# VectorE's read of each unit's first product, moved ahead of a stationary tile's low part

## The chip, the cores and the metric

The kernel runs on one core of one Trainium2 chip. The metric is the device time of one launch in microseconds (us), the median of several runs. Five engines work beside each other on the core: TensorE (PE; PEld is its weight load), VectorE (DVE), ScalarE (ACT), GpSimd (POOL) and SyncE (SP, here only a queue of transfers). They meet at semaphores alone.

## The reference

One layer of a decoder trunk on x (256 tokens, 2048 features), all float32:

```python
h = _rmsnorm(x, norm_mix)
b, c, xt, v = split(h @ w_in)                    # 4 x 1024 columns
y_conv = b * causal_depthwise_conv3(c * xt)
y_pool = pool_scale * group_linear(trailing_mean_w(v) - v)
x = x + concat(y_conv, y_pool) @ w_out
h = _rmsnorm(x, norm_mlp)
u = relu(h @ w_up)                               # 2048 -> 8192
x = x + (u * u) @ w_down                         # 8192 -> 2048
return _rmsnorm(x, norm_final)
```

The change lies in the last two products, the MLP.

## The kernel before, in words

**Arithmetic.** Every float32 operand is split in two parts for TensorE: ScalarE copies it to a reduced type (the high part, `w_hi` for a chunk of weights), VectorE subtracts that from the original (the low part, `w_lo`). A product is then high by high, high by low and low by high. A chunk of weights is 128 x 2048 (1 MB). There are four slots for chunks; an item of the stream has slot g % 4. ScalarE's `hi_of` (L793) waits until TensorE has used the item four places earlier (`chunk_used`), VectorE's `lo_of` (L1175) waits for ScalarE's high part, TensorE waits for both.

**The MLP.** The 8192 columns of `w_up` are 16 blocks `t` of 512; each takes 4 chunks, `("up", t, 0)` to `("up", t, 3)` (high parts L397, low parts L400), in banks 0 to 3. From block 2 on, TensorE also works off a unit `d = t - 2` of the down projection, 14 units in all. A unit is Strassen's scheme in Winograd's form: seven products instead of eight, each 128 tokens by 512 columns, on quadrants of `w_down` and on sums of them. They are called `s7_t3`, `a11_b11`, `n6_t2`, `a12_b21`, `s5_t1`, `a22_t4` and `n3_b22`; each is one call of `term` on TensorE, 8 matmuls with the high weights (L579 and L581 in turn) and 4 with the low ones (L585). The weights of such an item are a quadrant, or a sum in `mix_mem` that GpSimd adds up by accumulating transfers (L371) and by one tensor operation (L381). The stationary tiles are in `quads` (`act_b`), eight of them, S7, A11, N6, S5, A12, N3, A22 and A21, each with a high part (ScalarE, `quad_hi`, L818) and a low part (VectorE, `quad_lo`, L1194). Two units share one set: in units with even d ("folding" in the code) VectorE makes most of the set, and in odd ones only what the next set starts with.

**The order on TensorE** in unit d: up chunk 0, a11_b11, up chunk 1, n6_t2, a12_b21, up chunk 2, s7_t3 of unit d+1, s5_t1, up chunk 3, a22_t4, n3_b22. For d = 0 its own s7_t3 stands in front of a11_b11.

**Folding.** a11_b11, n6_t2, s5_t1 and n3_b22 of a unit grow in one PSUM bank (NT, that is bank 4). After each of them VectorE reads the bank and adds it to or subtracts it from the residual `x`: `fold` (L1205). So TensorE may not begin n6_t2 before VectorE has folded a11_b11:

```python
up_chunk(t, 1)
pe.wait_ge(folded, fold_count(d, "a11_b11"))
term("n6_t2", d, N6, NT, False)
```

All folds are counted by one semaphore, in VectorE's order. s7_t3 has a bank of its own (5 or 6), which a22_t4 goes on with.

**Order by hand.** Nothing plans the order: each engine's list is written out, and an engine does its list strictly in turn. SyncE's list is tied to VectorE's: a load into a slot of `w_raw` waits until VectorE has made the low part of what lay there. In unit d these are, in turn, up chunk 0, the quadrant in slot 2, up chunk 1, the base of the next sum, the quadrant for a12_b21 in slot 3, up chunks 2 and 3, and the quadrant for n3_b22 in slot 3, which waits for a12_b21's low part. GpSimd's list waits for the low parts of s7_t3, a11_b11 and n6_t2.

Of the kernel before, what the change touches and what calls it, by code (L numbers as in the profile page):

```python
# [15 lines left out]
NT = 4  # L16
# [63 lines left out]
def build(nc, x_t, x_rows, w_stream, w_quads, pool_w, params, g_final, out):  # L80
    F32, F32R = mybir.dt.float32, mybir.dt.float32r
    ALU, ACT = mybir.AluOpType, mybir.ActivationFunctionType

    ctx = ExitStack()
    with ctx:
# [142 lines left out]
        def fold_count(d, term):  # L228

            if term == "s7_t3":  # L230
                return 1 if d == 0 else fold_count(d - 1, "a12_b21") + 1
            if d + 1 < SEVENS:
                ends = {"s5_t1": 5, "n3_b22": 6, "a22_t4": 7}
            else:
                ends = {"s5_t1": 4, "a22_t4": 5, "n3_b22": 6}
            return 1 + 7 * d + ({"a11_b11": 1, "n6_t2": 2, "a12_b21": 3} | ends)[term]
# [5 lines left out]
        def x_quad(d, t, n):  # L242

            at = BLOCK_COLS * (2 * (d % 2) + n)
            return x[:, t, at:at + BLOCK_COLS]

        def bank_b(d):
            return NT + 1 + d % 2
# [661 lines left out]
        def _(dve):  # L910
# [262 lines left out]
            def lo_of(g, raw):  # L1173
                dve.wait_ge(hi_ready, g + 1)
                dve.tensor_tensor(out=w_lo[:, g % 4, :], in0=raw, in1=w_hi[:, g % 4, :].bitcast(F32),  # L1175
                                  op=ALU.subtract).then_inc(lo_ready, 1)

            def up_lo(t, c):
                lo_of(ITEM["up", t, c], w_raw[:, c % 2, :])

            def add_up(t):

                to = up_values(t)
                dve.wait_ge(cross_ready, IN_CROSSES + t + 1)
                dve.tensor_tensor(out=to[:, :, :], in0=bank_halves(1 if t == 1 else 0, 0),  # L1185
                                  in1=cross[:, :, :], op=ALU.add).then_inc(summed, 1)
                dve.wait_ge(summed, turn(FIRST_UP) + t + 1)
                dve.wait_ge(inv_rms_ready, 2)
                dve.scalar_tensor_tensor(out=to[:, :, :], in0=to[:, :, :], scalar=0.0, in1=by_token(),  # L1189
                                         op0=ALU.max, op1=ALU.mult).then_inc(value_ready, 1)  # L1190

            def quad_lo(s, g, src):
                dve.wait_ge(quad_hi_ready, quad_count(s, g))
                dve.tensor_tensor(out=quad_lo_of(g), in0=src, in1=quad_hi_of(g).bitcast(F32),  # L1194
                                  op=ALU.subtract).then_inc(quad_ready, 1)
                dve.wait_ge(quad_ready, quad_count(s, g))

            def fold(term, d, bank, t, n, op):

                dve.wait_ge(chunk_used, ITEM[term, d] + 1)  # L1200
                count = fold_count(d, term)
                if count > 1:
                    dve.wait_ge(folded, count - 1)
                to = x_quad(d, t, n)
                dve.tensor_tensor(out=to, in0=to, in1=ps[:, bank, :], op=op).then_inc(folded, 1)  # L1205
# [3 lines left out]
            def made(op):  # L1209
                op.then_inc(part_ready, 1)  # L1210
                parts[0] += 1
                dve.wait_ge(part_ready, parts[0])

            def make_s7():
                made(dve.tensor_tensor(out=part_2, in0=held[:, :, 0:P], in1=held[:, :, P:S],
                                       op=ALU.subtract))
# [9 lines left out]
            for t in range(LEAD, UPS):  # L1226
                d, s = t - LEAD, (t - LEAD) // 2
                folding = d % 2 == 0
                if d:
                    fold("s5_t1", d - 1, NT, 1, 1, ALU.subtract)  # L1230
                up_lo(t, 0)
                if d == 0:
                    lo_of(ITEM["s7_t3", 0], sums[0])
                add_up(t - 1)
                lo_of(ITEM["a11_b11", d], w_raw[:, 2, :])
                dve.wait_ge(squared, t)
                if folding:
                    made(dve.tensor_tensor(out=part_0, in0=val[:, :, P:S], in1=held[:, :, P:S],
                                           op=ALU.subtract))
                    made(dve.scalar_tensor_tensor(out=part_1, in0=held[:, :, 0:P], scalar=-1.0,  # L1240
                                                  in1=part_0, op0=ALU.mult, op1=ALU.subtract))
                elif s + 1 < SLICES - 1:
                    make_s7()
                if d:
                    fold("n3_b22", d - 1, NT, 0, 1, ALU.subtract)
                up_lo(t, 1)
                if d:
                    fold("a22_t4", d - 1, bank_b(d - 1), 1, 0, ALU.add)
                if folding:
                    quad_lo(s, N6, part_1)  # L1250
                    quad_lo(s, S5, part_0)
                    made(dve.scalar_tensor_tensor(out=part_1, in0=part_1, scalar=-1.0,
                                                  in1=val[:, :, 0:P], op0=ALU.mult, op1=ALU.subtract))
                elif s + 1 < SLICES - 1:
                    quad_lo(s + 1, S7, part_2)
                else:
                    quad_lo(s + 1, A21, held[:, :, P:S])
                dve.wait_ge(t2_added, d + 1)
                lo_of(ITEM["n6_t2", d], sums[d % 2])
                if folding:  # L1260
                    quad_lo(s, A12, val[:, :, 0:P])
                lo_of(ITEM["a12_b21", d], w_raw[:, 3, :])
                if d == 0:
                    fold("s7_t3", 0, bank_b(0), 1, 1, ALU.subtract)
                fold("a11_b11", d, NT, 0, 0, ALU.add)
                if folding:
                    quad_lo(s, N3, part_1)
                    quad_lo(s, A22, val[:, :, P:S])
                else:
                    quad_lo(s + 1, A11, held[:, :, 0:P])  # L1270
                up_lo(t, 2)
                if d + 1 < SEVENS:
                    lo_of(ITEM["s7_t3", d + 1], sums[(d + 1) % 2])
                fold("n6_t2", d, NT, 1, 0, ALU.add)
                lo_of(ITEM["s5_t1", d], w_raw[:, 2, :])
                fold("a12_b21", d, NT + 3, 0, 0, ALU.add)
                up_lo(t, 3)
                lo_of(ITEM["a22_t4", d], sums[d % 2])
                if d + 1 < SEVENS:
                    fold("s7_t3", d + 1, bank_b(d + 1), 1, 1, ALU.subtract)  # L1280
                lo_of(ITEM["n3_b22", d], w_raw[:, 3, :])
# [105 lines left out]
```

## Time and profile before

| | |
|---|---|
| median of 3 runs | 973.25 us (970.35, 973.25, 974.61) |
| profiled execution, its own time | 970.65 us |
| its span, first to last instruction | 968.9 us |
| PE busy | 950.2 us (98%) |
| DVE busy | 782.1 us (81%) |
| ACT busy | 526.8 us (54%) |
| POOL busy | 116.3 us (12%) |
| share of the DMA engines in the stretch of the units | 0.89 to 0.91 |
| granted TensorE clock | 0.998 of full speed |

1.75 us of the profiled execution lie outside its span. TensorE's row is almost full, but its matmuls overlap in the records, so busy time alone does not say how dense the stream is; the spacing of starts does. The units take the time from about 335 us to 917 us.

### The profile page before, as it was taken

How to read it: one execution, taken by the hardware profiler on the slowest of the kernel's cores; microseconds unless marked ns; L12 is line 12 of the kernel's file. 1: busy time of each engine (PE TensorE's matmuls, PEld its weight loads, DVE VectorE, ACT ScalarE, POOL GpSimd, SP SyncE). 2: the span in 40 equal slices, each digit the busy share in tenths (PEclk: the TensorE clock that was granted, in tenths of full speed). 3: DMA queues.
4: the chain of work that ended last, by engine and by line, in shares of the span. 5: the costliest groups of instructions: out<-in, count | busy, mean ns of one | idle time of the engine just before them, and what ended most of it. 6: DMA issues, size and time to landing. Idle time of an engine off the chain costs nothing.

```text
span 968.9 us, 12019 instructions
## 1 busy us (share of the span) xinstructions
PE 950.2 (98%) x4920; PEld 815.6 (84%) x4920; DVE 782.1 (81%) x605; ACT 526.8 (54%) x420; POOL 116.3 (12%) x65
## 2 busy tenths in 40 slices
PE   8999999999999999999999999999999999999996
PEld 7888888888888878888888888888888888888885
DVE  6597768664555699899999989989998998998864
ACT  6754335344444566465665556556555655646642
POOL 0000000000000203203020220203212030230000
PEclk9999999999999999999999999999999999999999
DMA  9956452655547598898979889898998989878832
GB/s 341 401 186 249 159 203 93 239 202 189 175 174 247 184 295 245 288 263 265 317 253 293 238 290 278 274 322 238 301 246 274 296 268 315 239 240 225 307 119 88
DMA packets 35763, 237.85 MB, mean 245 GB/s; under 512 B 3968, under 2 KB 4224, under 8 KB 7808
## 3 DMA queue, kind: packets, MB, share of 16 engines
q1 hardware_dynamic: 29232, 190.85, 51.0%
q0 software_dynamic: 6192, 45.09, 23.9%
q10 hardware_dynamic: 288, 1.18, 0.3%
q8 instruction: 37, 0.61, 0.2%
q14 instruction: 14, 0.11, 0.0%
HBM read 235.01 MB, written 2.10 MB: 245 GB/s over the span
## 4 chain that ended last, share of the span: by engine, by line
PE 73%; DVE 11%; issue 11%; DMA 2%; ACT 2%; SPq 0%; ACTq 0%; DVEq 0%
PE ps L397 26%; PE ps L400 14%; PE ps L488 9%; PE ps L579 6%; PE ps L581 6%; PE ps L585 6%; PE ps L623 4%; DVE w_lo L1175 3%; DMA w_raw<-w_stream 2%; DVE x L1205 2%; DVE act_b L1194 1%; ACT w_hi L793 1%; DVE val L1189 1%; DVE val L1185 1%; DVE w_lo L1009 1%
## 5 line engine op out<-in xcount | busy, mean ns | idle before, releaser
L397 PE MATMUL ps<-act_a,w_hi 128*128 128x512 f32 x1472 | 349.7, 390 | 0.0
L1175 DVE TENSOR_TENSOR w_lo<-w_raw,w_hi 128x2048 fp32r<-128x2048 f32 x120 | 324.3, 2702 | 8.3 <-ACT w_hi L793 7.2
L397 PEld LDWEIGHTS ps<-act_a,w_hi 128*128 128x128 f32 x1472 | 274.1, 188 | 55.5
L793 ACT ACTIVATE w_hi<-w_raw 128x2048 fp32r<-128x2048 f32 x120 | 229.4, 1913 | 76.5 <-PE ps L585 53.3
L400 PEld LDWEIGHTS ps<-act_a,w_lo 128*128 128x128 f32 x1472 | 188.6, 191 | 7.0
L400 PE MATMUL ps<-act_a,w_lo 128*128 128x256 f32 x1472 | 191.1, 283 | 0.0
L914 DVE TENSOR_TENSOR w_lo<-w_raw,w_hi 128x2048 fp32r<-128x2048 f32 x52 | 118.5, 2290 | 67.1 <-ACT w_hi L656 66.4
L579 PE MATMUL ps<-w_hi,act_b 128*128 128x512 f32 x392 | 153.9, 393 | 7.3 <-DVE x L1205 7.3
L581 PE MATMUL ps<-w_hi,act_b 128*128 128x512 f32 x392 | 153.3, 391 | 0.0
L656 ACT ACTIVATE w_hi<-w_raw 128x2048 fp32r<-128x2048 f32 x52 | 99.0, 1912 | 63.8 <-PE ps L400 39.0
L1175 DVE TENSOR_TENSOR w_lo<-mix_mem,w_hi 128x2048 fp32r<-128x2048 f32 x42 | 96.2, 2291 | 40.3 <-ACT w_hi L793 39.8
L793 ACT ACTIVATE w_hi<-mix_mem 128x2048 fp32r<-128x2048 f32 x42 | 80.2, 1910 | 80.1 <-PE ps L400 77.4
L381 POOL TENSOR_TENSOR mix_mem<-mix_mem,w_raw 128x2048 f32<-128x2048 f32 x14 | 78.4, 5598 | 249.7 <-DMA w_raw<-w_quads 226.1
L585 PE MATMUL ps<-w_lo,act_b 128*128 128x512 f32 x392 | 104.8, 389 | 0.0
L579 PEld LDWEIGHTS ps<-w_hi,act_b 128*128 128x128 f32 x392 | 73.8, 188 | 22.4 <-DVE x L1205 8.7
L585 PEld LDWEIGHTS ps<-w_lo,act_b 128*128 128x128 f32 x392 | 73.6, 188 | 15.3
L581 PEld LDWEIGHTS ps<-w_hi,act_b 128*128 128x128 f32 x392 | 73.8, 188 | 13.9
L1205 DVE TENSOR_TENSOR x<-x,ps 128x512 f32<-128x512 f32 x98 | 66.7, 680 | 3.0 <-PE ps L585 2.4
L488 PE MATMUL ps<-w_hi,act_b 128*128 128x512 f32 x256 | 68.8, 390 | 0.0
L371 POOL DMA_DIRECT2D mix_mem<-w_quads x28 | 24.5, 876 | 359.1 <-DMA mix_mem<-w_quads 262.5
L488 PEld LDWEIGHTS ps<-w_hi,act_b 128*128 128x128 f32 x256 | 47.8, 188 | 9.7
L807 ACT ACTIVATE cross<-ps 128x1024 f32<-128x1024 f32 x16 | 16.4, 1026 | 54.6 <-PE ps L400 54.6
(103 smaller groups left out, 589.0 us busy)
## 6 DMA issues: line engine op xcount, KB each, us to landing
w_raw<-w_stream SPq DMA_DIRECT2D x108, 1024.0 KB, 6.5
w_raw<-w_quads SPq DMA_DIRECT2D x50, 1024.0 KB, 8.8
mix_mem<-w_quads POOLq DMA_DIRECT2D x28, 1024.0 KB, 10.2
mix_mem<-w_quads SPq DMA_DIRECT2D x14, 1024.0 KB, 4.7
w_raw<-w_quads POOLq DMA_DIRECT2D x14, 1024.0 KB, 10.5
w_raw<-w_stream SPq DMA_DIRECT2D x16, 256.0 KB, 8.2
x<-x_rows SPq DMA_DIRECT2D x2, 1024.0 KB, 15.8
mix_mem<-x_t SPq DMA_DIRECT2D x3, 512.0 KB, 8.5
```

Of the source, the lines that this page charges most:

```text
L381: pool.tensor_tensor(out=sums[d % 2], in0=sums[d % 2], in1=w_raw[:, 2, :], op=ALU.add)\
L397: return pe.matmul(ps[:, bank, :], weights_hi, act, start=first, stop=False)
L400: return pe.matmul(ps[:, bank, 0:S], weights_lo, act[:, 0:S], start=False, stop=last)
L488: mm = pe.matmul(ps[:, NT * parity + t, :], a[:, at:at + P], cols, start=first and i == 0, stop=last and i == 2)
L579: pe.matmul(to, quads[:, quad, k, 0:P], weights_of(w_hi, g, k), start=first and k == 0, stop=False, skip_group_check=not first)
L581: pe.matmul(to, quads[:, quad, k, P:2 * P], weights_of(w_hi, g, k), start=False, stop=False, skip_group_check=not first)
L585: mm = pe.matmul(to, quads[:, quad, k, 0:P], weights_of(w_lo, g, k), start=False, stop=k == CK - 1, skip_group_check=not first)
L656: act.activation(w_hi[:, c, :], w_raw[:, c, :], ACT.Copy).then_inc(hi_ready, 1)
L793: act.activation(w_hi[:, g % 4, :], raw, ACT.Copy).then_inc(hi_ready, 1)
L914: dve.tensor_tensor(out=w_lo[:, c, :], in0=w_raw[:, c, :], in1=w_hi[:, c, :].bitcast(F32), op=ALU.subtract)\
L1175: dve.tensor_tensor(out=w_lo[:, g % 4, :], in0=raw, in1=w_hi[:, g % 4, :].bitcast(F32), op=ALU.subtract).then_inc(lo_ready, 1)
L1205: dve.tensor_tensor(out=to, in0=to, in1=ps[:, bank, :], op=op).then_inc(folded, 1)
```

## The change

In VectorE's list of a unit, the fold of a11_b11 moves up. Before, it stood behind the low part of tile A12 (in even units) and behind the low part of a12_b21's weights; now it stands directly behind the low part of n6_t2's weights. In unit 0 alone the fold of s7_t3, which has to stay ahead of it because of the common count, moves further, to behind the low part of up chunk 1. No instruction is added or removed, and the lists of the other engines stay as they are.

```diff
                 up_lo(t, 1)
                 if d:
                     fold("a22_t4", d - 1, bank_b(d - 1), 1, 0, ALU.add)
+                else:
+                    fold("s7_t3", 0, bank_b(0), 1, 1, ALU.subtract)
                 if folding:
                     quad_lo(s, N6, part_1)
                     quad_lo(s, S5, part_0)
...
                 dve.wait_ge(t2_added, d + 1)
                 lo_of(ITEM["n6_t2", d], sums[d % 2])
+                fold("a11_b11", d, NT, 0, 0, ALU.add)
                 if folding:
                     quad_lo(s, A12, val[:, :, 0:P])
                 lo_of(ITEM["a12_b21", d], w_raw[:, 3, :])
-                if d == 0:
-                    fold("s7_t3", 0, bank_b(0), 1, 1, ALU.subtract)
-                fold("a11_b11", d, NT, 0, 0, ALU.add)
                 if folding:
                     quad_lo(s, N3, part_1)
                     quad_lo(s, A22, val[:, :, P:S])
```

## Rows read from the trace of the kernel before

**Rows 1.** Waits of TensorE, whole span: total us, times, longest us.
```profile
PE ps L579 <- DVE x L1205: 7.3, 7, 2.0
```

**Rows 2.** Windows from stall to stall, first and last of six: length, busy us by engine.
```profile
348.26:432.01 83.75, 82.88 (x424) 70.94 (x424) 77.05 (x52) 48.31 (x34) 15.73 (x8) 1.00 0.91 279
...
767.11:850.92 83.81, 82.92 (x424) 70.94 (x424) 77.10 (x52) 49.42 (x34) 17.33 (x8) 1.00 0.89 276
```

**Rows 3.** Timeline of TensorE in unit 2: start us, us of the merged row.
```profile
420.78 2.08 PE L400 MATMUL ps<-act_a,w_lo 128*128 128x256 f32 x16
422.69 0.40 PE L579 MATMUL ps<-w_hi,act_b 128*128 128x512 f32 x1
...
424.54 1.07 PE L585 MATMUL ps<-w_lo,act_b 128*128 128x512 f32 x4
...
429.07 2.07 PE L400 MATMUL ps<-act_a,w_lo 128*128 128x256 f32 x16
432.01 0.50 PE L579 MATMUL ps<-w_hi,act_b 128*128 128x512 f32 x1 [0.88 <-DVE x L1205]
...
433.99 1.08 PE L585 MATMUL ps<-w_lo,act_b 128*128 128x512 f32 x4
```

**Rows 4.** Timeline of VectorE in unit 2.
```profile
420.56 0.69 DVE L1205 TENSOR_TENSOR x<-x,ps 128x512 f32<-128x512 f32 x1
...
426.14 2.29 DVE L1175 TENSOR_TENSOR w_lo<-mix_mem,w_hi 128x2048 fp32r<-128x2048 f32 x1
428.35 0.69 DVE L1194 TENSOR_TENSOR act_b<-val,act_b 128x512 fp32r<-128x512 f32 x1
...
431.28 0.68 DVE L1205 TENSOR_TENSOR x<-x,ps 128x512 f32<-128x512 f32 x1
431.88 0.69 DVE L1194 TENSOR_TENSOR act_b<-cross,act_b 128x512 fp32r<-128x512 f32 x1
```

**Rows 5.** Timelines of TensorE and of VectorE in unit 0.
```profile
337.88 0.39 PE L579 MATMUL ps<-w_hi,act_b 128*128 128x512 f32 x1
...
344.23 2.07 PE L400 MATMUL ps<-act_a,w_lo 128*128 128x256 f32 x16
348.26 0.50 PE L579 MATMUL ps<-w_hi,act_b 128*128 128x512 f32 x1 [1.96 <-DVE x L1205]
339.42 1.41 DVE L1194 TENSOR_TENSOR act_b<-cross,act_b 128x512 fp32r<-128x512 f32 x2
343.80 0.69 DVE L1194 TENSOR_TENSOR act_b<-val,act_b 128x512 fp32r<-128x512 f32 x1
```

**Rows 6.** Unit 3: VectorE's low part, ScalarE released by a11_b11, TensorE's n6_t2.
```profile
468.67 2.29 DVE L1175 TENSOR_TENSOR w_lo<-w_raw,w_hi 128x2048 fp32r<-128x2048 f32 x1
468.19 0.63 ACT L818 ACTIVATE act_b<-win 128x512 fp32r<-128x512 f32 x1 [0.83 <-PE ps L585]
473.47 0.40 PE L579 MATMUL ps<-w_hi,act_b 128*128 128x512 f32 x1
```

**Rows 7.** Idle times of VectorE later on, from its timeline.
```profile
361.58 2.29 DVE L1175 TENSOR_TENSOR w_lo<-mix_mem,w_hi 128x2048 fp32r<-128x2048 f32 x1 [1.93 <-ACT w_hi L793]
445.38 2.29 DVE L1175 TENSOR_TENSOR w_lo<-mix_mem,w_hi 128x2048 fp32r<-128x2048 f32 x1 [1.96 <-ACT w_hi L793]
```

**Rows 8.** A low part while GpSimd adds; GpSimd's addition, min/median/max ns.
```profile
405.70 6.11 DVE L1175 TENSOR_TENSOR w_lo<-w_raw,w_hi 128x2048 fp32r<-128x2048 f32 x1
L381 POOL TENSOR_TENSOR mix_mem<-mix_mem,w_raw x14: 4617/5526/6595, 327.9 to 864.4; 128x2048 f32<-128x2048 f32 x14
```

**Rows 9.** SyncE's load for n3_b22 in unit 2; SyncE's quadrant loads to landing; TensorE's n3_b22.
```profile
431.39 0.33 SPq L315 DMA_DIRECT2D w_raw<-w_quads  x1
DMA to landing us min/median/max: 4.6/7.3/12.6
456.92 0.39 PE L579 MATMUL ps<-w_hi,act_b 128*128 128x512 f32 x1
```

**Rows 10.** ScalarE's longest wait for a transfer, 400 to 920 us.
```profile
ACT w_hi L793 <- DMA mix_mem<-w_quads: 2.7, 1, 2.7
```

## The prediction

> **What bounds the kernel now.** I read the page's first two parts, then the waits by engine, the windows, and last the timelines of TensorE and VectorE around one place. TensorE's row is full nearly everywhere, so the first question is where it stands still. The view of TensorE's waits has one entry of size: 7.3 us in 7 pieces, all ahead of a term's first matmul (L579) and all ended by a fold (L1205) [rows 1]. The longest, 2.0 us, lies in unit 0; the other six lie at about 0.9 us in units 2, 4, ..., 12. Odd units have none. From one of them to the next the windows are 83.75 to 83.81 us long, all six alike [rows 2]: a period of two units that TensorE's work sets, plus one stall.
>
> The timeline says which fold it is. In unit 2 the low half of up chunk 1 starts at 429.07, and the next matmul, the first of n6_t2, at 432.01 [rows 3]. VectorE's fold there runs from 431.28 to 431.96 [rows 4]; by the order of its list it is that of a11_b11. TensorE goes on 0.05 us after its end. VectorE is not waiting at that point: from the low part of n6_t2's weights at 426.14 on it works without a break. The fold is late only because two other instructions stand ahead of it, A12's low part at 428.35 and that of a12_b21's weights right behind.
>
> **What a stall costs.** A chunk's 16 low matmuls take 1.91 us from their first start to the next instruction's (420.78 to 422.69), so without the wait n6_t2 would begin at 429.07 + 1.91 = 430.98. It begins at 432.01: 1.03 us late. Its first eight matmuls then need 433.99 - 432.01 = 1.98 us where an undisturbed term needs 424.54 - 422.69 = 1.85; the pipeline fills anew, 0.13 us [rows 3]. Together 1.16 us. In unit 0, 344.23 + 1.91 = 346.14 against 348.26 is 2.12 us [rows 5], with the same 0.13 us 2.25 us. Sum: 6 x 1.16 + 2.25 = 9.2 us, if every stall goes fully.
>
> **Does the fold come early enough, in even units?** It now takes the place of A12's low part: start 428.35 [rows 4]. It may start, since a11_b11 was through before up chunk 1 began. Duration 0.68 us, end 429.03, and 0.05 us later TensorE knows. TensorE arrives at 430.98, so 1.90 us are to spare. The stall does not shrink, it goes, and VectorE could be that much later before it came back.
>
> **Unit 0.** Here the fold of s7_t3 goes ahead too. It starts at 339.42, where the low part of N6 started; s7_t3 was through when TensorE began a11_b11 at 337.88, so it does not wait. A fold moves what follows by 0.60 us (431.28 to 431.88 [rows 4]). The low part of n6_t2's weights, followed before by A12's at 343.80, is then done at 344.40, and the fold of a11_b11 runs from 344.40 to 345.08. TensorE arrives at 346.14 [rows 5]: 1.0 us to spare. I count the whole 2.25 us.
>
> **Odd units.** The fold moves ahead of a12_b21's low part, to 468.67. a11_b11 ended just before: ScalarE was released by it at 468.19 [rows 6]. So VectorE passes the wait with 0.48 us in hand. Were it earlier by more than that, it would wait for TensorE, but TensorE needs the fold only at 473.47, more than 4 us after it. Nothing gained, nothing lost.
>
> **What is late next.** What the fold overtakes comes 0.60 us later, and TensorE 1.03 to 1.16 us earlier than before. (1) A12's low part starts at 428.95 and is done at 429.64; a12_b21 begins behind all of n6_t2, whose first eight matmuls alone take 1.85 us, so not before 430.98 + 1.85 = 432.83. (2) The low part of a12_b21's weights runs from 429.67 to 431.96 at 2.29 us; its first use is 1.85 us into the term, not before 434.68: at least 2.7 us to spare. (3) Behind both, VectorE's list is at the same time as before, 431.88, for the sum of durations is unchanged; against TensorE it is 1.16 us later. That lag does not pile up: at 445.38, in the same unit, VectorE has been idle for 1.96 us, ended by ScalarE, which follows TensorE's use of the slots [rows 7]. The idle time becomes 0.8 us and the two stand to each other as before. In unit 0 the idle time is 1.93 us at 361.58 against 2.25 us of gain; 0.3 us of lag go into unit 1. (4) The nearest other fold, that of n3_b22, ends at 421.25 [rows 4] for a term that begins at 422.69 [rows 3], 1.4 us; it hangs on the standing at the last common point and does not move. So nothing in the even unit takes the stall's place, and in unit 1 the 0.3 us fit in 1.4.
>
> **Transfers.** One of them hangs on a moved instruction: SyncE loads n3_b22's quadrant when a12_b21's low part is done, at 431.39 in unit 2 [rows 9], so at 432.0 now. SyncE's entries behind it wait for later low parts that don't move. TensorE begins n3_b22 at 456.92 before, 455.8 now, and needs its low part 1.85 us in, at 457.6. Going back over 6.11 us for a disturbed low part [rows 8] and, generously, as much again for ScalarE's copy ahead of it, the load must land by 445.4, 13.4 us from its issue; the slowest of SyncE's quadrant loads took 12.6 us [rows 9]. GpSimd's orders wait for the low parts of s7_t3, a11_b11 and n6_t2; only in unit 0 is one (n6_t2's) later, by 0.60 us.
>
> **GpSimd beside VectorE.** In each unit one low part takes some 6.1 us where others take 2.29; it lies beside GpSimd's addition, which takes 4.62 us undisturbed [rows 8]. The transfers that start the addition follow VectorE, and the waits that VectorE is held by follow TensorE, so the addition moves by up to 1.16 us against VectorE's list and may fall on the next item. The price by rows: VectorE is held for 3.83 us now and can be held for at most one whole addition, 4.62 us, so 0.8 us more, within the 1.4 us of (4). I take nothing, and keep 0.8 - 0.8 = 0 as the lower and, for six pairs where the margin has gone, 6 x 0.8 = 4.8 us as the upper bound.
>
> The Trainium skill ("Trainium Architecture — The Big Picture", What this means for kernel authors) calls the SBUF port pair of VectorE and GpSimd an exclusive lock and not a split of bandwidth. The trace agrees (6.11 us in place of 2.29 us); by that rule the later of the two waits for the other, and the sum stays at 9.2 us as long as one addition meets one low part per unit. The rule speaks against the change only if the addition got in ahead of n6_t2's low part, and its time is elsewhere in the unit.
>
> **Sum.** 970.65 - 9.2 = 961.4 us for the profiled execution. It is at the low end of the runs shown; from their median, 973.25, it is 964.0. The four executions' middle is 972.0, which gives 962.8. I take 963.5.
>
> **Rivals.**
> (A) All stalls go, as above: 963.5 us, 961 to 966 with the scatter of the runs. Chance 0.76.
> (B) The lag shows elsewhere. VectorE loses 1.16 us per pair against TensorE and has 1.96 us of idle time to absorb it; if the addition above takes its 0.8 us more, nothing is left, and TensorE stands at the following fold or sum. Then some 0.8 us of 1.16 come back in each pair, 4.8 us in all: 968.3 us. For it: the 0.3 us of unit 1. Against: the 1.4 us that must go first. Chance 0.12.
> (C) The transfers pace the units, with the DMA engines 0.89 to 0.91 busy [rows 2]. Then the six stalls are time that would be waited for anyway, and only unit 0's 2.25 us is won: 971.0 us. Against it: the longest wait of ScalarE for a transfer in over 500 us is 2.7 us, once [rows 10]. A fold that is not the last release, so that TensorE stays where it is, would look the same. Chance 0.08.
> (D) Slower: the later load of n3_b22. If that load, not TensorE, set the pace, each of 14 units would get 0.60 us longer and the stalls' end would win nothing: 973.25 + 8.4 = 981.7 us. It decides once the load takes over 13.4 us, against 12.6 at most. Chance 0.04.
>
> **Range and chances.** 0.5% is 4.9 us, about what a measurement of this kernel tells from no change. The range reaches from 960.0 (A from the lowest run, 970.35 - 9.2 = 961.2, and a little scatter) to 968.5, which takes in B; C and D and the ends of A's scatter are left out. Faster by over 0.5%: A, and half of B, whose 4.9 us lie on the line: 0.82. Within 0.5%: the other half, C: 0.14. Slower: D, 0.04.
>
> **What the profile after would show.** Right: no entry of L1205 in TensorE's waits; six windows of 82.6 us between the starts of n6_t2 in even units; the fold of a11_b11 at 0.68 us directly behind n6_t2's low part; VectorE's idle time in even units 0.8 us in place of 1.96; its busy time the same. B would show new waits of TensorE for VectorE and a low part beside the addition over 6.5 us; C, waits of ScalarE for transfers, and windows still near 83.8; D, ScalarE's wait ahead of n3_b22. The prediction is wrong if another semaphore was the late one in the stall, or if VectorE's idle time is not there when the stall is gone.

## The result and the profile after

The changed kernel takes 961.78 us (median of 6 runs: 961.26, 961.37, 961.63, 961.93, 964.38, 964.45), the kernel before beside it 972.83 us (6 runs, 970.35 to 974.87). The ratio is 0.9896, 95% interval 0.9875 to 0.9916, so the change is worth 8.2 to 12.2 us. Forecast were 963.5 us, in a range from 960.0 to 968.5, and a sum of 9.2 us.

TensorE's waits after, whole span (line and releaser, total us, times, longest us), beside the one entry of [rows 1]:

```profile
PE ps L462 <- DVE val L921: 2.9, 1, 2.9
PE ps L422 <- DVE w_lo L1009: 1.2, 2, 0.8
PE ps L521 <- POOL win L364: 1.0, 1, 1.0
```

The entry of the folds is gone; what is left lies ahead of the MLP, before 50 us. The kernel before waits at the same three lines, for 2.0 us at L422, 1.0 us at L521 and, at L462:

```profile
PE ps L462 <- DVE val L921: 0.3, 1, 0.3
```

The windows from one even unit to the next, first and last of six, show what that gives (bounds, length, busy us of PE, PEld, DVE, ACT, POOL, clock, DMA share, GB/s):

```profile
347.16:429.77 82.61, 82.61 (x425) 70.89 (x424) 77.86 (x54) 50.49 (x34) 15.24 (x9) 1.00 0.92 285
...
760.23:842.84 82.61, 82.61 (x426) 70.89 (x424) 77.08 (x52) 49.42 (x34) 15.99 (x9) 1.00 0.92 279
```

Length and TensorE's busy time are now the same number, 82.61; before, 0.9 us were missing in each [rows 2], and they were 83.75 to 83.81 us long. The same place of unit 2 on TensorE:

```profile
429.77 2.08 PE L400 MATMUL ps<-act_a,w_lo 128*128 128x256 f32 x16
431.69 0.40 PE L579 MATMUL ps<-w_hi,act_b 128*128 128x512 f32 x1
...
433.53 1.07 PE L585 MATMUL ps<-w_lo,act_b 128*128 128x512 f32 x4
```

From the low half to n6_t2 it is 1.92 us, where it was 2.94 us [rows 3], and n6_t2's first eight matmuls take 1.84 us, not 1.98. VectorE there, and its idle time later in the unit:

```profile
426.86 2.29 DVE L1175 TENSOR_TENSOR w_lo<-mix_mem,w_hi 128x2048 fp32r<-128x2048 f32 x1
429.07 0.68 DVE L1205 TENSOR_TENSOR x<-x,ps 128x512 f32<-128x512 f32 x1
429.67 0.69 DVE L1194 TENSOR_TENSOR act_b<-val,act_b 128x512 fp32r<-128x512 f32 x1
...
444.91 2.29 DVE L1175 TENSOR_TENSOR w_lo<-mix_mem,w_hi 128x2048 fp32r<-128x2048 f32 x1 [0.77 <-ACT w_hi L793]
```

The fold ends at 429.75, 1.94 us ahead of the matmul that needs it. The idle time is 0.77 us where it was 1.96 us [rows 7]. From the low half of up chunk 1 in unit 0 (347.16 after, 344.23 before) to that of the last up chunk (903.44 after, 909.72 before) the units take 556.28 us instead of 565.49 us: 9.21 us less.

The profiled execution as a whole, 964.38 us against 970.65 us, shows only 6.3 us less, because it reached the units 2.9 us later. That comes from the wait at L462, which is not where the change was made. The wait ends 1.5 us later than in the kernel before's trace (48.15 us against 46.63), and the lower clock behind it costs the rest: the next high half starts at 52.07 us against 49.09, 3.0 us later. Runs 10 to 12 below are about it.

### The profile page after: what moved, and what is told of

It is laid out like the page before. It is cut to its first block, busy times and chain, and to the rows that moved or that the text cites. A ratio compares the mean times of both kernels' runs of the same rounds, so it can differ in the third digit from the quotient of the medians.

```text
span 962.6 us, 12019 instructions
## 1 busy us (share of the span) xinstructions
PE 949.4 (99%) x4920; PEld 816.6 (85%) x4920; DVE 782.5 (81%) x605; ACT 526.9 (55%) x420; POOL 113.0 (12%) x65
## 4 chain that ended last, share of the span: by engine, by line
PE 94%; DMA 3%; DVE 2%; SPq 1%; ACT 0%; issue 0%; ACTq 0%
PE ps L397 34%; PE ps L400 18%; PE ps L581 9%; PE ps L579 9%; PE ps L585 9%; PE ps L488 9%; PE ps L623 5%; DMA w_raw<-w_stream 3%; DVE w_lo L1009 1%; SPq L295 0%; PE ps L422 0%; PE ps L474 0%; DVE act_a L964 0%; DVE w_lo L914 0%; ACT w_hi L656 0%; SPq L280 0%
## 5 line engine op out<-in xcount | busy, mean ns | idle before, releaser
L397 PE MATMUL ps<-act_a,w_hi 128*128 128x512 f32 x1472 | 349.7, 390 | 0.0
L397 PEld LDWEIGHTS ps<-act_a,w_hi 128*128 128x128 f32 x1472 | 274.1, 188 | 55.5
L381 POOL TENSOR_TENSOR mix_mem<-mix_mem,w_raw 128x2048 f32<-128x2048 f32 x14 | 75.1, 5367 | 248.7 <-DMA w_raw<-w_quads 225.2
```

What stands on the lines that cost most here:

```text
L381: pool.tensor_tensor(out=sums[d % 2], in0=sums[d % 2], in1=w_raw[:, 2, :], op=ALU.add)\
L397: return pe.matmul(ps[:, bank, :], weights_hi, act, start=first, stop=False)
```

## The experiments

### Which units pay: runs 1 to 3

Run 1 moves the fold in even units alone, run 2 in unit 0 alone, run 3 in odd units alone. In all three the code behind n6_t2's low part is

```diff
-                fold("a11_b11", d, NT, 0, 0, ALU.add)
+                moved = folding                    # run 2: d == 0; run 3: not folding
+                if moved:
+                    fold("a11_b11", d, NT, 0, 0, ALU.add)
                 if folding:
                     quad_lo(s, A12, val[:, :, 0:P])
                 lo_of(ITEM["a12_b21", d], w_raw[:, 3, :])
+                if not moved:
+                    if d == 0:
+                        fold("s7_t3", 0, bank_b(0), 1, 1, ALU.subtract)
+                    fold("a11_b11", d, NT, 0, 0, ALU.add)
```

and in run 3 the early fold of s7_t3 is taken out too.

> The fold of a11_b11 is moved in even units alone (unit 0 with its s7_t3 fold); in odd units it stays behind the low part of a12_b21's weights. My theory (only even units had a stall, so only they gain): the same as the changed kernel, 9 to 10 us below the kernel before, no wait of TensorE for a fold, windows of 82.6 us from n6_t2 to n6_t2 of the next even unit. Rival (VectorE's order in odd units shares in the gain, or costs): more than 1 us off the changed kernel, seen as windows other than 82.6 us.

961.67 us, ratio to the kernel before 0.9903 (0.9881 to 0.9925), 10.5 us less by the medians, a little over the 9 to 10 expected. No wait for a fold; windows of 82.61 us, and 556.28 us from unit 0 to the last up chunk, as in the changed kernel. The even units are the whole of it.

> Both folds are moved in unit 0 alone. Theory: of the seven stalls one goes, the one of 2.25 us; six waits of TensorE of 0.9 us each stay in units 2, 4, ..., 12 and the windows stay at 83.75 to 83.8 us; time 2 to 2.5 us below the kernel before (about 970.5). Rival C (transfers pace the even units, and only unit 0's share is real): this kernel is as fast as the changed one, 962.

968.62 us, ratio 0.9966 (0.9953 to 0.9978), so 3.6 us less by the medians and not the 2 to 2.5 us expected. In the trace, though, all is as expected: the first window, unit 0 to unit 2, is 82.62 us, the others stay at 83.77, and the way from unit 0 to the last up chunk is 563.21 us, 2.28 us less than before. Rival C, that transfers pace the even units, falls: with their stalls left in, the kernel is 6.8 us slower than the changed one. What did not fit was the median. It came with another thing: these six executions lay between 968.35 and 968.80 us, while those of the kernel before, measured beside them, were spread over 3.9 us (970.55 to 974.47). The fastest of each are 2.2 us apart, as expected; the surplus lies in the slower executions of the kernel before.

> The fold is moved in odd units alone; in even units all stands as in the kernel before. Theory: no gain and no loss, all seven waits stay (7.3 us), time as before within 0.2%. Rival (VectorE, held up for TensorE's a11_b11 by the moved fold, gets later): VectorE idle before L1205 in odd units, and longer stalls in the even units behind them.

972.18 us, ratio 1.000 (0.9988 to 1.0011), all seven waits at 7.3 us. But its trace takes 567.01 us from unit 0 to the last up chunk, with the same waits as the kernel before with 565.49 us. The 1.5 us lie directly behind unit 0's stall. TensorE's timeline there:

```profile
348.17 0.66 PE L579 MATMUL ps<-w_hi,act_b 128*128 128x512 f32 x1 [1.96 <-DVE x L1205]
348.62 0.63 PE L581 MATMUL ps<-w_hi,act_b 128*128 128x512 f32 x1
349.04 0.63 PE L579 MATMUL ps<-w_hi,act_b 128*128 128x512 f32 x1
349.47 0.63 PE L581 MATMUL ps<-w_hi,act_b 128*128 128x512 f32 x1
```

and the windows around it, where the third number from the right is the granted clock:

```profile
347.00:348.00 1.00, 0.00 (x0) 0.00 (x0) 0.90 (x2) 1.00 (x1) 0.00 (x0) 1.00 1.05 188
348.00:349.00 1.00, 0.83 (x2) 0.69 (x3) 0.96 (x3) 0.22 (x1) 0.00 (x0) 0.68 0.90 156
349.00:350.00 1.00, 1.00 (x4) 0.77 (x3) 0.97 (x2) 0.00 (x0) 0.00 (x0) 0.50 0.90 180
350.00:351.00 1.00, 1.00 (x4) 0.81 (x3) 1.00 (x1) 0.00 (x0) 0.00 (x0) 0.50 1.05 246
351.00:352.00 1.00, 1.00 (x4) 0.77 (x4) 1.00 (x2) 0.00 (x0) 0.00 (x0) 0.62 0.91 238
352.00:353.00 1.00, 1.00 (x6) 0.83 (x5) 1.00 (x1) 0.14 (x1) 0.00 (x0) 1.00 1.01 279
```

TensorE has stood for 1.96 us; some 0.2 us after it goes on, the clock is at 0.50, the lower of its two levels (1.2 GHz), and the matmuls start 0.43 us apart instead of 0.23 us, eight times over, 1.6 us in sum. From this stretch's low half to that of unit 2 it is 86.43 us (344.14 to 430.57), in the kernel before's trace, with the same stall at full clock, 84.84 us (344.23 to 429.07): 1.59 us.

### Unit 0's stall alone: run 4

The changed kernel, with `moved = d > 0` in the code of run 1 and s7_t3's fold back in its old place.

> The changed kernel with unit 0 alone put back: there both folds stand where the kernel before had them, so its stall of 2.0 us is back and no other. In the run with the fold moved only in odd units, TensorE's granted clock stood at 0.50 for some 3 us right behind that stall, and the matmuls there started 0.43 us apart in place of 0.23 us; the kernel before's own trace has the same stall at full clock. Theory (the stall in unit 0 costs 2.25 us always, and 1.6 us more in the executions in which the clock drops to the lower level behind it): runs between 963.5 and 965.5, median 964 to 965.5, more scattered than the changed kernel; 6 to 8 us below the kernel before. Rival (the stall costs its 2.25 us and the scatter has its place elsewhere): median 963.7, scatter as in the changed kernel.

965.51 us (963.56, 963.87, 965.31, 965.71, 965.75, 966.48), ratio 0.9924 (0.9907 to 0.9941). The profiled execution is the fastest, 963.56 us, with the stall of 2.0 us and the clock at 1.00 behind it; it is 2.3 us above the fastest of the changed kernel (961.26). The median is 3.7 us above the changed kernel's, between the 2.25 us of the stall alone and the 3.85 us with the lower clock behind it; the scatter ahead of the units (runs 10 to 12 below) is in it too. The rival's 963.7 us is missed by the median, not by the fastest executions. Three executions lie above the 965.5 us expected as the upper end. In the trace the way from unit 0 to the last up chunk is 558.54 us (344.08 to 902.62), 2.26 us more than in the changed kernel: that is the price of this stall at full clock, 2.25 us forecast.

So the stall costs its length always, and more in most executions. That the clock is what the slower four lost is likely and not shown: the run's one trace is of the fastest. The mean granted clock on record for each execution points that way, 0.998 in the two fastest and 0.994 to 0.997 in the other four. But it is a mean over the whole execution, and it can't tell where the clock was low: run 1's fastest execution has 0.995, and its trace shows the lower clock between 8 and 12 us and again behind 945 us, with no loss in the units.

### How much room there is: runs 5 to 8

Run 5 puts the fold behind A12's low part, still ahead of the weights' low part:

```diff
                 lo_of(ITEM["n6_t2", d], sums[d % 2])
-                fold("a11_b11", d, NT, 0, 0, ALU.add)
                 if folding:
                     quad_lo(s, A12, val[:, :, 0:P])
+                fold("a11_b11", d, NT, 0, 0, ALU.add)
                 lo_of(ITEM["a12_b21", d], w_raw[:, 3, :])
```

> In all units the fold stands behind A12's low part but still ahead of the low part of a12_b21's weights: 0.72 us later in even units than in the changed kernel. Theory (1.90 us to spare in even units, 1.0 us in unit 0): the same time as the changed kernel, no wait of TensorE for a fold. Rival (the margin is smaller than worked out from starts and ends): waits of TensorE for L1205 come back, in unit 0 first.

961.45 us, ratio 0.9891 (0.9875 to 0.9908), no wait for a fold, windows of 82.61 us. It is the overtaking of the weights' low part that counts; A12's is not in the way.

Runs 6 to 8 add work to VectorE that nothing uses, a sum over 128x1024 elements (1.22 us by the traces; two of them, with the gap behind, 2.50 us), to an otherwise unchanged kernel:

```diff
+            def extra(n):
+                for _ in range(n):
+                    dve.tensor_reduce(out=ballast[:, :], in_=by_token(), axis=mybir.AxisListType.X,
+                                      op=ALU.add).then_inc(extra_done, 1)
...
+                if folding:
+                    extra(1)          # run 7: extra(2); run 8: extra(2), behind the fold
                 fold("a11_b11", d, NT, 0, 0, ALU.add)
```

> The changed kernel with one more VectorE instruction, a sum of 128x1024 elements that nothing uses, some 1.1 to 1.3 us, ahead of the moved fold in each even unit. Theory (1.90 us to spare in even units, 1.0 us in unit 0): no wait in units 2 to 12, one of 0.1 to 0.3 us in unit 0; time within 0.5 us of the changed kernel. Rival (the margin worked out from the rows is too large): waits of TensorE for L1205 in every even unit.

962.49 us, ratio 0.9895 (0.9874 to 0.9916); no recorded wait for a fold, the windows from unit 2 on 82.62 us. The median is 0.7 us above the changed kernel's, where 0.5 was expected. From unit 0 to unit 2 it is 83.20 us, 0.59 us more than in the changed kernel. Some 0.35 us of it are at the fold: n6_t2 begins at 346.68, 0.25 us after the 344.52 + 1.91 at which it could, and refills for 0.10 us. The other 0.24 us lie ahead of unit 1's first up chunk, which waits for VectorE's sum: the sum ends at 374.31 and TensorE begins at 374.37 instead of 374.27, and refills. It is the place at which run 8 loses its time.

> Two such instructions ahead of the moved fold in each even unit, some 2.4 us, more than the 1.90 us to spare. Theory: the stalls come back at 0.4 to 0.6 us each in six units and 1.4 us in unit 0, each with 0.13 us of refill: 4 to 6 us above the changed kernel. Rival (VectorE has room and TensorE would wait elsewhere): the same time as the changed kernel, or waits in odd units too and more than 8 us.

968.34 us, ratio 0.9957 (0.9945 to 0.9969): 6.6 us above the changed kernel, 4 to 6 expected. TensorE's waits (TensorE's lines are two higher in this kernel, the fold's is L1216):

```profile
PE ps L581 <- DVE x L1216: 4.8, 7, 1.3
```

The timelines of VectorE and of TensorE in its unit 2, the added work first:

```profile
428.67 2.47 DVE L1204 TENSOR_REDUCE ballast<-inv_rms 128x4 f32<-128x1024 f32 x2
431.17 0.69 DVE L1216 TENSOR_TENSOR x<-x,ps 128x512 f32<-128x512 f32 x1
429.09 2.07 PE L402 MATMUL ps<-act_a,w_lo 128*128 128x256 f32 x16
431.91 0.50 PE L581 MATMUL ps<-w_hi,act_b 128*128 128x512 f32 x1 [0.75 <-DVE x L1216]
```

All seven stalls are back. In units 6 to 12 they are 0.47 us by the record and 0.6 us by the starts, as 2.50 - 1.90 gives, and the windows there are 83.37 us, 0.75 us up (0.6, and 0.13 of refill). In units 2 and 4 they are 0.3 us longer than forecast: there VectorE also comes later into the unit.

> The same two instructions directly behind the moved fold in even units, so that the fold is on time and everything after it in VectorE's list is some 2.4 us later. Rival B of the prediction at work: VectorE's idle time of 0.8 us later in the unit is used up and some 1.6 us of lag go into the odd unit, where 1.4 us are to spare ahead of the up chunk that waits for VectorE's sum. Theory: no wait of TensorE in even units, waits of 0.2 to 0.4 us in the six or seven odd ones; 1 to 3 us above the changed kernel. Rival (the lag is absorbed in full): the same time as the changed kernel.

966.97 us, ratio 0.9939 (0.9918 to 0.9960): 5.2 us above the changed kernel, against 1 to 3 expected. The fold is on time and TensorE stands instead in the odd units, ahead of the up chunk that waits for VectorE's sum (the chunk's line, L399 here, is L397 in the changed kernel). The view of the waits holds four of the stalls; by the starts there is one in each of the seven odd units:

```profile
PE ps L399 <- DVE win L1187: 1.9, 4, 1.0
```

In the steady pairs the price is as worked out: windows of 83.03 to 83.15 us, 0.4 to 0.5 us up. Taking 0.13 us of refill off 0.42 leaves 0.29; so of 2.50 us, 0.77 went into idle time and 2.50 - 0.77 - 0.29 = 1.44 us into the room ahead of the sum, 1.4 us forecast. The theory missed the ends: 1.3 us are lost behind unit 0, which has no idle time left, 1.0 us at the end of unit 2, where a low part beside GpSimd's addition takes 6.67 us, and 0.9 us behind unit 12. This is the mechanism of rival B, which needed 2.5 us of added work to show at all.

### The load of n3_b22: run 9

```diff
-                load_quad(w_raw[:, 3, :], d, 3, ITEM["a12_b21", d], raw_loaded[3])
+                load_quad(w_raw[:, 3, :], d, 3, ITEM["up", t, 2], raw_loaded[3])
```

> The changed kernel, but SyncE's load for n3_b22 waits for the low part of up chunk 2 instead of a12_b21's, so it is issued 3 to 4.5 us later in every unit. Rival D of the prediction (a later load of n3_b22 sets the pace) would make every one of 14 units longer: over 40 us in all. Theory (the load has at least 13.4 us, and needs 12.6 at most): time within 0.3% of the changed kernel, windows of 82.6 us, perhaps a longer wait of ScalarE for the transfer.

962.09 us, ratio 0.990 (0.9873 to 0.9927). In unit 2 the load is issued 6.6 us behind the start of up chunk 1's low half (433.39 against 426.80) where the changed kernel issues it 2.9 us behind (432.71 against 429.77), 3.7 us later; the windows stay at 82.61 us. Rival D falls.

### The wait ahead of the units: runs 10 to 12

In run 10 TensorE spreads the first norm (L462) behind the high half of chunk 3 of its block instead of chunk 2; run 12 is the same kernel again, beside run 11, which is the changed kernel again.

```diff
-            gemm_block(1, act_a, 1, norm=0, norm_after=11)
+            gemm_block(1, act_a, 1, norm=0, norm_after=15)
```

> The changed kernel, but the spreading of the first norm by TensorE (L462), where TensorE stood for 2.9 us in the changed kernel's profiled execution with the clock at 0.50 behind it, stands behind the high half of chunk 3 of block 1 instead of chunk 2. Theory: this wait is what separates the executions near 964.4 us from those near 961.5 us; without it all runs lie within 1 us, at 960.5 to 961.8. Rival (VectorE and ScalarE now wait for the norm some 5 us longer, and their later work on the pool branch holds TensorE up): 1 to 5 us slower than the changed kernel, with waits of TensorE in the blocks behind.

960.50 us (959.96, 960.36, 960.63, 960.87), ratio 0.9875 (0.9851 to 0.9899). TensorE has no wait at L462 and none that is new; VectorE stands 4.8 us for what follows the norm, and TensorE does not wait for that.

> The changed kernel once more, beside the next run on the same chip. So far one execution in four of it and of its near copies lay near 964 us and the others at 961 to 962. Theory (the wait at the first norm, and the lower clock behind it, come in some executions): the same picture, median 961.5 to 962, one or two executions at 963.5 or more.

962.58 us (961.20, 962.57, 962.58, 964.04), ratio 0.9905 (0.9888 to 0.9922), 0.6 us above the upper end of what was expected for the median. The profiled execution, 962.57 us, waited 1.4 us at L462.

> The changed kernel with the first norm's spreading behind chunk 3's high half, once more. Theory: no execution over 961.5 us, median 960.3 to 960.8, 1.0 to 1.5 us below the changed kernel in the same call, and TensorE's row without a wait at L462. Rival (the four executions so far were lucky): the same scatter as the changed kernel, executions near 963 to 964 among them.

960.63 us (960.13, 960.30, 960.97, 961.28), ratio 0.9886 (0.9870 to 0.9903), 1.95 us below run 11, measured beside it, where 1.0 to 1.5 were expected; no wait at L462. No execution of the eight went over 961.28 us, while 8 of the 22 of the changed kernel and of the copies with the same units (runs 1, 5, 9, 11) were at 962.5 us or more.

What a long wait there does is in the changed kernel's own trace, first in TensorE's timeline:

```profile
48.15 1.22 PE L462 MATMUL ps<-inv_rms,ones 128*128 128x128 f32 x4 [2.87 <-DVE val L921]
49.03 3.21 PE L400 MATMUL ps<-act_a,w_lo 128*128 128x256 f32 x16
```

and then in the windows of the same stretch:

```profile
46.00:48.00 2.00, 0.00 (x0) 0.00 (x0) 1.90 (x6) 2.00 (x2) 0.00 (x0) 1.00 1.01 422
48.00:50.00 2.00, 1.85 (x8) 1.85 (x9) 1.82 (x2) 0.76 (x3) 0.00 (x0) 0.50 0.77 320
```

2.87 us of waiting, then the clock at 0.50 and a low half of 3.21 us that takes 2.08 us elsewhere. What makes VectorE late there in some executions was not followed further; in this trace the two low parts ahead of the norm start 1.5 us later than in the kernel before's (40.37 against 38.84). The profiled executions line up with it: a wait of 0.7 us or less in three at 961.17 to 961.40 us (runs 1, 5 and 9), 1.4 us in run 11 at 962.57, 2.9 us with the lower clock at 964.38. The start of up chunk 1's low half in unit 0 makes it exact: an execution's time less that start is 617.21 or 617.22 us in all seven traces of these units (the changed kernel, runs 1, 5, 9, 10, 11 and 12) and 626.42 us in the kernel before's. So what these seven differ by, 960.30 to 964.38 us, lies wholly ahead of the units, and the change itself is 9.2 us in each.

## Why the prediction was right

**Which fold, and what a stall costs.** Right. With the fold moved no such wait is left, and the sum of 6 x 1.16 + 2.25 = 9.2 us stands against 9.21 us in the traces. The parts are confirmed one by one: windows shorter by 1.16 us (83.77 to 82.61), and unit 0's stall worth 2.28 us in run 2, where it alone is taken out, and 2.26 us in run 4, where it alone is left in. The 0.13 us of refill, which the view of the waits doesn't hold, is part of both.

**Unit 0 and even units: room for the fold.** Right. 1.90 us forecast, 1.94 us seen from the fold's end to the matmul, 0.05 us of which are the signal; run 6 fits within, run 7 does not, and what it loses is the difference in units 6 to 12. In unit 0 the fold ends at 348.01 where TensorE would come at 349.07; the 1.0 us forecast is what run 6 used up.

**Odd units.** Right: run 3 gains nothing, run 1 loses nothing.

**What is late next.** Right for this change, with less in hand than forecast in one place (below, under GpSimd). VectorE's idle time fell to 0.77 us, 0.8 forecast, and unit 0's to none. Run 8 shows the next limit where it was put, 1.4 us ahead of the sum that an odd unit's first up chunk waits for. I had read these 1.4 us off the fold of n3_b22, which comes later in the list; the sum is as tight: it ends at 416.46 in the changed kernel's unit 2, and the chunk begins at 417.86.

**GpSimd.** The forecast that the addition may fall on the next item held, and it cost TensorE nothing: in VectorE's timeline at the ends of units 0 and 4 (here unit 4's) the low part of n3_b22 is now undisturbed and the one behind it, of the next up chunk, is held.

```profile
530.33 2.29 DVE L1175 TENSOR_TENSOR w_lo<-w_raw,w_hi 128x2048 fp32r<-128x2048 f32 x1
...
533.12 6.11 DVE L1175 TENSOR_TENSOR w_lo<-w_raw,w_hi 128x2048 fp32r<-128x2048 f32 x1
```

It was not free for VectorE. In unit 2 the low part beside the addition takes 6.60 us, where the same one took 5.90 us before, and the sum behind it ends at 458.46 with TensorE's chunk beginning at 459.17: 0.71 us are left of the 1.4 us. A low part of over 6.5 us was named as a sign of rival B; here it came without a wait of TensorE, and runs 6 and 8 show the waits that a low part of 6.66 and 6.67 us brings once VectorE is later.

```profile
447.93 6.60 DVE L1175 TENSOR_TENSOR w_lo<-w_raw,w_hi 128x2048 fp32r<-128x2048 f32 x1
...
457.25 1.21 DVE L1185 TENSOR_TENSOR win<-ps,cross 128x1024 f32<-128x1024 f32 x1
```

**Transfers.** Right: rivals C and D fell with runs 2 and 9.

**What the sum left out.** The medians differ by 11.05 us, not 9.2, and the interval takes both in. The fastest executions of all, 970.35 and 961.20 us, differ by 9.15 us. A term that the sum lacks is a second price of unit 0's stall: the lower clock behind it, 1.59 us in the one trace that has it. Run 2, which removes that stall alone, won 3.6 us by the medians against 2.28 us in its trace, and its executions agree to 0.5 us. The prediction had the stall at full clock in its one trace and took its length for its whole cost. That the clock accounts for the whole 1.3 us of difference in run 2 is likely, but each run has only one trace; it isn't shown execution by execution, the wait at L462 may have a part in the scatter of the kernel before too, and run 2's interval (2.1 to 4.6 us) holds 2.28 too. And 963.5 us, put between a sum from the profiled execution (961.4) and one from the median (964.0), was 1.7 us high; that it lay so near owes something to the choice between the two.

## What to carry to other kernels

When an engine that should never stand waits for a short instruction on another engine, look at what stands ahead of that instruction there: if the queue in front of it is busy with work not needed until later, the order is the fault, and the gain is the stall plus the refill, read from starts. Before trusting it, find the place where the helping engine next waits for the busy one; its idle time there is the cover that keeps the lag from piling up, and together with the room ahead of the next handover (0.8 and 1.4 us here, 0.7 us at its tightest) it says how much more could be asked. Last, the best kernel here is run 10's, the change with the first norm spread one chunk later, 960.5 us and, measured again as run 12, 960.6 us. Where executions scatter, compare the waits of several traces: a stall that comes in some executions only can be moved like a constant one.

## What the runs showed of the hardware

A stall of TensorE of 1.96 us was followed by full clock in two traces (the kernel before, run 4) and by a granted clock of 0.50 between 348.4 and 351.6 us in a third (run 3), with the same work before and after; the six stalls of 0.9 us in the traces of the kernel before, of run 2 and of run 3 had full clock behind them. At 2.87 us, ahead of the units in the changed kernel, it dropped as well, and so it did for some 3 us behind waits of 1.87 us (run 1) and 2.25 us (run 2) at L422, at 8 us of their traces; behind a wait of 1.61 us there, in run 11, it stayed full. So unit 0's stall costs 2.2 us in one execution and 3.8 us in another.

GpSimd's addition of two 128x2048 tiles takes 4.6 us when VectorE leaves it alone, and VectorE's subtraction of two such tiles in SBUF, beside it, 6.1 us instead of 2.29 us, ending some 2.15 us after the addition's end: in the changed kernel's unit 2, the addition gets in under a fold at 405.80, which reads PSUM, and the subtraction behind waits it out.

```profile
405.26 5.11 POOL L381 TENSOR_TENSOR mix_mem<-mix_mem,w_raw 128x2048 f32<-128x2048 f32 x1 [18.44 <-DMA w_raw<-w_quads]
405.80 0.68 DVE L1205 TENSOR_TENSOR x<-x,ps 128x512 f32<-128x512 f32 x1
406.40 6.12 DVE L1175 TENSOR_TENSOR w_lo<-w_raw,w_hi 128x2048 fp32r<-128x2048 f32 x1
```

The addition ends at 410.37, 4.57 us after the fold's start and not after its own: by these times it was held by the low part ahead from 405.26 to 405.80. Twelve of the fourteen additions in this trace end 4.55 to 4.59 us after the start of a fold, though their own records are 4.61 to 6.50 us long. That is the lock that the Trainium skill ("Trainium Architecture — The Big Picture", What this means for kernel authors) describes; the trace agrees, and adds that a fold is the gap through which GpSimd takes it.
